# Transposes of a norm's result inside the preceding product, between its hi and lo parts, and the DVE and ACT work around the norms in another order

## The reference

```python
x = x + merged @ w_out[l]                                  # block 1, end of its mixer
h2 = rms_norm(x, g_mlp[l])
x = x + jnp.square(jax.nn.relu(h2 @ w_up[l])) @ w_down[l]
...
mix = jnp.einsum('bsc,cd->bsd', mixed, w_out)              # each of the two layers
x = layernorm(DEEPNORM_ALPHA * x + mix, ln1_g, ln1_b)
hid = jnp.square(jax.nn.relu(jnp.einsum('bsd,df->bsf', x, w_ff1)))
ff = jnp.einsum('bsf,fd->bsd', hid, w_ff2)
return layernorm(DEEPNORM_ALPHA * x + ff, ln2_g, ln2_b)
```

## Time and profile before

| | |
|---|---|
| median of 3 runs | 1271.27 us (1271.05 to 1272.31) |
| the profiled execution | 1271.03 us |
| its span, first to last instruction | 1269.2 us |
| PE busy | 1225.7 us, 97% of the span |
| DVE busy | 769.7 us, 61% |
| ACT busy | 608.6 us, 48% |
| mean granted clock of PE | 0.997 |

### The profile page before, as it was taken

The page is one execution under the profiler, slowest core; times in us unless marked ns, Lnnn a source line. Parts: engine busy times, 40 slices in busy tenths (PEclk is TensorE's granted clock), DMA queues, the critical chain, the costliest instruction groups (busy, mean ns, idle before and its releaser), DMA issues.

```text
span 1269.2 us, 18459 instructions
## 1 busy us (share of the span) xinstructions
PE 1225.7 (97%) x7568; PEld 1085.8 (86%) x7568; DVE 769.7 (61%) x853; ACT 608.6 (48%) x679; POOL 0.2 (0%) x4
## 2 busy tenths in 40 slices
PE   5999999999999999999989999999999999999997
PEld 4979998988888789899788878999988977899895
DVE  5566875674565665545366686555565677755555
ACT  4565554665444454444355445543435544544441
POOL 0000000000000000000000000000000000000000
PEclk9999999999999999999999999999999999999999
DMA  5644354444565355555253454645516345365550
GB/s 204 237 167 167 114 176 143 170 140 154 215 215 184 133 199 199 197 192 173 95 206 133 141 199 169 230 166 197 186 66 243 138 141 199 133 232 180 188 194 33
DMA packets 33533, 217.31 MB, mean 171 GB/s; under 512 B 4416, under 2 KB 6464, under 8 KB 7744
## 3 DMA queue, kind: packets, MB, share of 16 engines
q1 hardware_dynamic: 33472, 216.44, 48.1%
HBM read 215.37 MB, written 1.05 MB: 171 GB/s over the span
## 4 chain that ended last, share of the span: by engine, by line
PE 73%; DVE 12%; DMA 7%; ACT 5%; issue 2%; SPq 0%; ACTq 0%; DVEq 0%
PE gps L1291 27%; DMA raw<-w 7%; PE aps L1330 7%; PE aps L1331 7%; PE aps L1336 7%; PE gps L1330 6%; PE gps L1331 6%; PE gps L1336 6%; DVE w_lo L730 5%; ACT w_hi L335 3%; DVE B L878 1%; PE aps L1449 1%; DVE rs L868 1%; DVE B L872 1%; DVE B L822 1%
## 5 line engine op out<-in xcount | busy, mean ns | idle before, releaser
L730 DVE TENSOR_TENSOR w_lo<-raw,w_hi 128x2048 fp32r<-128x2048 f32 x200 | 449.1, 2249 | 292.7 <-ACT w_hi L335 291.6
L335 ACT ACTIVATE w_hi<-raw 128x2048 fp32r<-128x2048 f32 x200 | 374.9, 1877 | 233.2 <-DMA raw<-w 121.6
L1291 PE MATMUL gps<-R_hi,w_hi 128*128 128x256 f32 x736 | 192.5, 283 | 0.0
L1291 PE MATMUL gps<-R_hi,w_lo 128*128 128x256 f32 x736 | 192.3, 283 | 0.0
L1291 PE MATMUL gps<-H_hi,w_hi 128*128 128x256 f32 x640 | 172.7, 291 | 11.5 <-ACT H_hi L370 5.9
L1291 PE MATMUL gps<-H_hi,w_lo 128*128 128x256 f32 x640 | 169.3, 286 | 0.0
L1330 PE MATMUL aps<-w_hi,Q_hi 128*128 128x512 f32 x416 | 162.6, 391 | 2.4 <-DVE Q_lo L928 1.8
L1331 PE MATMUL aps<-w_lo,Q_hi 128*128 128x512 f32 x416 | 162.2, 390 | 0.0
L1291 PE MATMUL gps<-R_lo,w_hi 128*128 128x256 f32 x736 | 147.6, 283 | 0.0
L1291 PEld LDWEIGHTS gps<-R_hi,w_lo 128*128 128x128 f32 x736 | 141.2, 192 | 0.8
L1291 PEld LDWEIGHTS gps<-R_hi,w_hi 128*128 128x128 f32 x736 | 141.1, 192 | 0.8
(11 more groups left out here) (212 smaller groups left out, 1426.9 us busy)
## 6 DMA issues: line engine op xcount, KB each, us to landing
raw<-w SPq DMA_DIRECT2D x196, 1024.0 KB, 4.8
B<-rows SPq DMA_DIRECT2D x4, 1024.0 KB, 4.7
B<-x_t SPq DMA_DIRECT2D x2, 512.0 KB, 4.6
B<-mem_t SPq DMA_DIRECT2D x1, 1024.0 KB, 7.6
B<-x SPq DMA_DIRECT2D x1, 1024.0 KB, 7.5
B<-con SPq DMA_DIRECT2D x1, 1024.0 KB, 9.0
out<-B SPq DMA_DIRECT2D x4, 256.0 KB, 2.0
B<-rows SPq DMA_DIRECT2D x1, 512.0 KB, 6.9
```

What stands on the lines that cost most here:

```text
L335: act.activation(w_hi[:, ring(l), 0:n], raw[:, raw_slot(l), 0:n], ACT.Copy)\
L730: dve.tensor_tensor(w_lo[:, ring(l), 0:n], raw[:, raw_slot(l), 0:n], w_hi[:, ring(l), 0:n].bitcast(F32), ALU.subtract)\
L1291: return pe.matmul(gps[:, bank_, nt * T:(nt + 1) * T], w[:, r, c:c + P], op[:, k, :], start=start, stop=stop, skip_group_check=True)
```

## The change

The first chunk of a norm's result is transposed inside the last product before the norm, between that product's hi and lo parts; each further chunk is transposed inside the product of the chunk before it. `turn`, `turn_hi` and `turn_lo` now handle one chunk i = 2m + j. DVE and ACT take their work around the norms in another order to fit, and three splits change places. Nothing computed changes.

```diff
@@ PE
+                if between is not None:
+                    turn(*between)
                 if lo_ready is not None:
                     pe.wait_ge(*lo_ready)
...
             def tokens_after_norm(h0, l, n, banks, op_hi, op_lo, src, ready, count):
                 for m in range(2):
-                    turn(n, m, src, ready, count)
                     for g in range(2):
+                        i = 2 * m + g
                         pe.wait_ge(s["lo_ready"], h0 + (l + g + 1))
...
+                                          between=(n, i + 1, src, ready, count) if i < 3 else None)
...
-                            ins = tokens_part(l + a, acc(m, a), m, par_, Q_hi, Q_lo, stop=True)
+                            ins = tokens_part(l + a, acc(m, a), m, par_, Q_hi, Q_lo, stop=True,
+                                              between=after if m and a else None)
@@ ACT, site 1
+                squared(0, 0)
+                squared(0, 1)
+                root_start(0, 0)
+                turn_hi(N_MLP, 0, R_hi)
+                squared(1, 0)
+                turn_hi(N_MLP, 1, R_hi)
+                squared(1, 1)
+                root_start(0, 1)
+                turn_hi(N_MLP, 2, R_hi)
+                turn_hi(N_MLP, 3, R_hi)
@@ ACT, start of every MLP (DVE in the same way, with up_lo)
                 split(h0, l0 + 4)
-                split(h0, l0 + 5)
                 up_hi(n, ub, 0)
                 up_hi(n, ub, 1)
+                split(h0, l0 + 5)
@@ ACT, end of w_out in the layers, inside the loop over m
                             act.activation(operand(Q_hi, m, 1), four(retention_turned(m)), ACT.Copy)\
                                .then_inc(s["gn_hi"], 1)
-                        split(h0, LFFN)
-                        split(h0, LFFN + 1)
+                            split(h0, LFFN + m)
@@ DVE, site 1
                 turn_lo(N_MLP, 0, R_hi, R_lo)
                 added(1, 1)
+                turn_lo(N_MLP, 1, R_hi, R_lo)
                 rooted(1)
-                turn_lo(N_MLP, 1, R_hi, R_lo)
+                turn_lo(N_MLP, 2, R_hi, R_lo)
+                turn_lo(N_MLP, 3, R_hi, R_lo)
@@ DVE, layer norm, inside rooted(m)
                     finished(m, 0)
+                    if m and hi is not None:
+                        turn_lo(i, 1, hi, lo)
                     centred(m, 1)
                     st.settle()
                     finished(m, 1)
@@ DVE, site 2
+            ended(0, 0)
+            ended(0, 1)
+            ended(1, 0)
+            turn_lo(N_END, 0, H_hi, H_lo)
+            ended(1, 1)
+            for i in range(1, 4):
+                turn_lo(N_END, i, H_hi, H_lo)
@@ DVE, end of w_out in the layers
                 gn_lo(0)
+                split(h0, LFFN)
                 gn_lo(1)
-                split(h0, LFFN)
                 split(h0, LFFN + 1)
```

More of the change, by code:

```diff
@@ L371, in rms_norm, with turn_hi @@
                        .then_inc(s["nhi"], 1)
[L373 to L378, removed]
+            def turn_hi(n, i, hi):
+                m, j = i // 2, i % 2
+                act.wait_ge(s["t_tr"], 4 * n + i + 1)
+                act.activation(operand(hi, m, j), four(turned(m, j)), ACT.Copy)\
+                   .then_inc(s["nhi"], 1)
             def root_start(i, m):
@@ L388, in mlp_norm, with squared @@
             def mlp_norm():
[L390 to L396, removed]
+                def squared(m, j):
+                    act.wait_ge(s["resid"], 2 * m + j + 1)
+                    act.activation(dump[:, j, :], chunk(X, m, j), ACT.Square, scale=1.0 / 32,
+                                   accum_out=stats[:, m, 20 + j:21 + j]).then_inc(s["t_sq"], 1)
+                squared(0, 0)
[8 more added lines that the diff above has]
+                turn_hi(N_MLP, 3, R_hi)
             def layer_norm(n, hi):
@@ L619, in _ @@
             ffn(0, FFN1, 0)
-            for m in range(2):
-                turn_hi(N_END, m, H_hi)
+            for i in range(4):
+                turn_hi(N_END, i, H_hi)
             split_gates(HALVES1, 0)
@@ L806, in root, with turn_lo @@
                 newton(v, r0, a, r, None)
[L808 to L814, removed]
+            def turn_lo(n, i, hi, lo):
+                m, j = i // 2, i % 2
+                dve.wait_ge(s["nhi"], 4 * (n + 2) + i + 1)
+                dve.tensor_tensor(operand(lo, m, j), four(turned(m, j)),
+                                  operand(hi, m, j).bitcast(F32), ALU.subtract)\
+                   .then_inc(s["nlo"], 1)
             def residual(m, j, out, scale):
@@ L1125, in _, with ended @@
             ffn(0, FFN1, 0)
[L1126 to L1130, removed]
+            def ended(m, j):
+                sum_done(N_END, m, j, HALVES1)
+                residual(m, j, acc(m, j), None)
+            ended(0, 0)
[5 more added lines that the diff above has]
+                turn_lo(N_END, i, H_hi, H_lo)
             for a in range(2):
@@ L1320, in tokens_part @@
             def tokens_part(l, out, m, g, op_hi, op_lo, start=False, stop=False, ks=range(4),
[L1321 removed]
+                            hi_ready=None, lo_ready=None, between=None):
                 r = ring(l)
@@ L1347, in tokens_half, with turn @@
                     .then_inc(s["gemm_done"], 1)
[L1349 to L1356, removed]
+            def turn(n, i, src, ready, count):
+                pe.wait_ge(ready, count + i + 1)
+                m, j = i // 2, i % 2
+                for k in range(4):
+                    ins = pe.transpose(turned(m, j)[:, k * P:(k + 1) * P],
+                                       chunk(src, m, j)[:, k * P:(k + 1) * P], ident)
+                ins.then_inc(s["t_tr"], 1)
             def turn_merged(j, m):
@@ L1383, in sum_tiles, with ffn @@
                 return ins
-            def ffn(h0, l0, n, src, ready, count):
+            def ffn(h0, l0, n, src, ready, count, after):
                 ub = 16 * n
@@ L1701, in w_out @@
                                               hi_ready=(s["gn_hi"], ly * 2 + m + 1),
-                                              lo_ready=(s["gn_lo"], ly * 2 + m + 1))
+                                              lo_ready=(s["gn_lo"], ly * 2 + m + 1),
+                                              between=(N_LN + 2 * ly, 0, X, s["t_z"], 4 * (1 + 2 * ly))
+                                              if m and a else None)
                             ins.then_inc(s["acc_ready" if m == 0 else "gemm_done"], 1)
```

18 lines of the change are left out of this document (11 added, 7 removed).

## The result

The changed kernel took **1275.43 us** (median of 6 runs, 1273.12 to 1276.39), the kernel before 1271.16 (6 runs, 1270.76 to 1272.53): ratio **1.0029** (1.0016 to 1.0042). The prediction was 1274.5. The profiled execution of the changed kernel is its shortest run, 1273.12 with a span of 1271.3, so its trace holds 2.1 us of the loss; the other five runs are 1.2 to 3.3 us longer than it.

What follows compares the result with a forecast made beforehand. PE, with work for 97% of the span, was taken as the bound. Site terms 1.2 + 1.1 + 0.3 + 1.45 - 0.55 gave +3.5 us on the profiled 1271.03: 1274.5, range 1269.5 to 1277.

Steps and rivals of the forecast that it cites:

- The likeliest case: Whole kernel: the site terms sum to +3.5 us, 1274.5; chance 0.55, own range +1.8 to +5.
- site 1: First norm, ahead of an MLP: `rows_first` starts at 451.0 against 449.70, +1.2 us; ends -0.1 and +1.5.
- rest of site 5: Last MLP site without the row load: `rows_first` 0.95 us later, but the Q_lo stop of 1.12 goes.
- What is late next: Ahead of each MLP: last transposes to `rows_first` take 5.51 us against PE's own 4.10, a new 1.4 us stop.
- T3: Start of a norm's last group of transposes, chunk (1, 1), moved from ahead of two products to inside the first.
- PE's own saving: At each norm: four transpose groups cost 1.88 us instead of 3.00, saving 1.12 a site, 5.6 in all.
- Sites 2 and 4: Norms ahead of the gates: 1 MB loads go out later behind late small splits, +1.1 and +1.45 us; the delay stays.
- rival (b): Gains and new stops nearly cancel, as with the gate loads' delay made up: +0.95 us, 1272.0; chance 0.24.
- Sites 3 and 5: Norms behind w_out, ahead of MLPs: `rows_first` later, but Q_lo stops of 0.63 and 1.12 go; +0.3 and -0.55 us.
- The row load at site 5: Row load issued later, so ACT's 0.82 us wait for half LFFN+1 shrinks: 0.4 gained, between 0 and 0.8.
- Site 4 already paid it and lost nothing.: Against a clock loss: the stretch behind site 4, with a clock fall, took 27.87 us, site 2's 27.81.
- rival (c): The clock also falls behind longer waits at sites 2 and 4: +3.2 us more if not absorbed, 1277.7; chance 0.08.

Runs made afterwards that it cites:

- e1: Changed kernel with half l0+2 split ahead of the last copy (DVE: last lo part) at sites 1, 3 and 5: 1271.30 us, ratio 1.0000.
- e2: Changed kernel with the gate halves' two small splits ahead of chunk (1,0)'s copy and lo part at sites 2 and 4: 1267.18 us, ratio 0.9968.
- e11: Kernel before with early gate splits and the change's three swapped splits, no transposes inside products, second run: 1263.89 us, ratio 0.9946.
- e12: Kernel before with only the change's three swapped splits, gate splits where they were: 1268.70 us, ratio 0.9976.
- e4: Kernel before with only the gate halves' splits moved ahead of the m = 1 copies and lo parts at sites 2 and 4: 1266.94 us, ratio 0.9966.
- e5: Changed kernel, unedited, measured and profiled a second time: 1276.11 us, ratio 1.0034.
- e10: Changed kernel with both half l0+2 and the gate halves split early, second run: 1264.05 us, ratio 0.9940.
- e8: Changed kernel with 40 unread identity transposes meant to fill PE's long waits at sites 2 and 4, placed one wait too late: 1278.37 us, ratio 1.0046.

## Why the prediction was right, and where its terms were off

The likeliest case came, 0.9 us above the predicted median. The mechanism is the one that was forecast; that the sum came so close is partly luck, for terms of both signs were too small. The stretches give the terms one by one:

| term | predicted | first profile | second profile |
|---|---|---|---|
| site 1 (stretch 1-2) | +1.2 | +1.06 | +1.07 |
| site 2 (2-3) | +1.1 | +1.27 | +2.43 |
| site 3 (3-4) | +0.3 | +0.06 | +0.98 |
| site 4 and the row load (4-5) | +1.05 | +0.47 | +0.88 |
| rest of site 5 (5-end) | -0.15 | -0.39 | -0.42 |
| span | +3.5 | +2.1 | +4.7 |

(The 0.4 for the row load lies ahead of site 5, so it stands with site 4 here. The profile of before started site 1 at 429.36, those of the changed kernel 0.3 to 0.4 earlier.)

- **What is late next.** Right. T3 to `rows_first` is 5.42 at sites 1, 3 and 5, against the 5.51 summed from rows. The stop is 1.21 by the distance of starts (listed as 1.04) instead of 1.4: PE starts 2.35 instead of 2.44 after `w_lo`, and its own work from T3 takes 4.21 and not 4.10. e1 shows the cause: moving this one split takes the loss of the MLP sites away.
- **PE's own saving.** Too large. Groups without a stop are 3.29 to 3.30 apart (434.55 to 437.84, 618.56 to 621.86), where I took 3.19: a group inside a product costs 0.57, because the matmuls behind it run slower at first (the lo part takes 1.02 instead of 0.91, and the hi part behind it 1.93 instead of 1.81). At site 2 the last lo part started at 631.75 before, 13.88 after the first one's start at 617.87, and now 631.73 - 618.56 = 13.17 after the first group: 0.71 saved, not 1.12. At site 1 the wait of 0.60 for chunk (1, 0) takes most of it.
- **Sites 2 and 4.** Right. The loads are 1.42 and 1.36 later against the first group (1.1 and 1.45 forecast), the waits 4.21 and 4.23. e2 shows the cause. The stretch behind takes back 0.4 of 3.84 at site 2 and nothing at site 4, so "the delay stays" holds for nine tenths, and rival (b) for little.
- **Sites 3 and 5.** The direction was right, the swap of l0+5 under-sized. I priced it by the stops for Q_lo as listed, 0.63 and 1.12. The list leaves out 0.26 of each: e11 and e12, without a fall of the clock, have 182.38 and 182.39 in stretch 3-4 against 183.32 before (0.94), and e11 has 180.97 in 5-end against 182.35 (1.38). At site 1 I took 0.1 for the stop, and it cost 0.39 (182.95 against 182.56).
- **The row load at site 5.** The size was too small, and the mechanism is in doubt. ACT's wait for half LFFN+1 didn't shrink from 0.82 but grew to 1.91, at both layers, because the split ahead of it now comes 3 us earlier. What PE sees of it shrank all the same: from w_out's last group of transposes L1670 (now L1694) to the residual add were 7.48 us at layer 0 and 8.02 at layer 1, and are 7.30 at both. So the first layer gives 0.18 and the second 0.72, where I took 0 and 0.4. e4, without the swap, has 7.48 at both layers, so 0.18 is the swap's and 0.54 was one late load, such as also came with the swap (7.97 in e5). That the row load made it late isn't shown: at layer 0 the row load went out at the same place in SP's list, and ACT's wait was 0.19.
- **"Site 4 already paid it and lost nothing."** This reading of rival (c) held for the sites it was made for. The waits of 4.4 us came (4.21 and 4.23), the clock fell behind both, and from the first matmul behind the wait to the transposes L1655 the first profile has 27.11 and 26.91, where the kernel before has 26.93 and 27.00. What the longer falls of the second profile (27.47 and 27.48) cost there isn't shown. What (c) left out is the wait for the first chunk at sites 3 and 5: a fall behind it costs 0.9 us. The Trainium skill (TensorE: Matmul & The Clock Gate, "Why this matters for your kernels") has PE at half clock again after an idle gap; the trace agrees at both sites behind waits of over 4 us, and behind shorter ones it fell in some executions and not in others. At site 3, behind the same two stops of 1.07 and 0.79, it stayed at 1.00 in the kernel before and fell to 0.50 in e4. So falls of the clock there and late loads are the likely reason for the longer runs of the changed kernel. That isn't shown run by run, for the other runs have only a mean clock (0.991 to 0.993, the profiled one 0.995).

Taken apart by e12, the change is a gain of 3.1 us from three swapped splits, and a loss of 7.4 (1276.11 - 1268.70) from the insertion with the orders that it brings. (The two medians come from two chips, whose medians of the kernel before are 0.3 us apart.) The terms of both signs were forecast at -2.2 and +5.7. Both were too small by about a quarter, and the errors cancelled for the most part in the sum.

## What to carry over

Before a piece of work is moved to a later place on one engine, look at what is queued behind its consumers on the others. Here it was a 1.9 us split that PE needs 5 us later, and two tiny splits that release loads of 1 MB; both could be put ahead of the copy, where the engine stood idle. When two things are changed at once (a structure and the orders around it), measure the orders alone: here they held all of the gain. And use events that no edit touches as a ruler, with the granted clock beside it: it tells 0.1 us in a stretch that PE alone sets, and some 0.5 in one that holds waits for loads, where medians tell 2.

## What the hardware showed beyond what was expected

- One kernel at one place, PE waiting 4.21 and 4.35 us at site 2: in one profile the clock fell half a microsecond after the wait, in the other two microseconds before its end, and it stayed down for 3.4 and for 7 us.
- What a fall costs depends on what stands behind it. Behind the wait for a chunk at sites 3 and 5, where PE goes on to long products, it cost 0.9 us each time. Behind the waits at sites 2 and 4, where loads of 1 MB are waited for next, a fall of 3.4 us cost nothing that can be seen (27.11 and 26.91 us with it, 26.93 to 27.67 without).
- PE has a wait near 82 us, in code that no experiment touches. In the profiles of before, of the changed kernel (both), of e2 and of e10 the clock stayed at 1.00 behind it (waits of 1.9, 2.0, 2.3, 2.5 and 2.3), and site 1 starts at 428.9 to 429.4. In eight others it fell (waits of 2.1 to 2.7), and site 1 starts at 430.4 to 431.4; in e8 the wait is 3.3, with a fall. The length of the wait alone doesn't decide it.
- A group of four 128-wide transposes put between 512-wide matmuls costs 0.57 us, 0.36 for itself and the rest in the matmuls behind it.
